# Two experts' rows kept on chip and added by TensorE; the other rows read back while the last expert runs

## Chip, core and metric

One NeuronCore of a Trainium2 chip runs the whole kernel in one launch. The metric is the device time of that launch in microseconds (us), the median of several runs. One further execution was taken with the hardware profiler; its rows are read here. TensorE is called PE, VectorE DVE, ScalarE ACT, GpSimd POOL and SyncE SP.

## What is computed

A two-layer encoder on 512 tokens of width 1024, all float32. Each layer mixes tokens (three kinds of attention and a convolution, one input and one output projection) and then runs a mixture of experts:

```python
for l in range(2):
    ...                                     # mixer: x = x + gt1 * mix
    h2 = rms_norm(x, g2) * (1 + sc2) + sh2
    # every token goes to 2 of 32 experts, with gates that sum to p_group
    y  = sum over its two experts e:  gate_e * ((silu(h2 @ Wg[e]) * (h2 @ Wu[e])) @ Wd[e])
    x  = x + gt2 * y
out = rms_norm(x, g_final)
```

Wg and Wu are 1024x512 and Wd is 512x1024, so one expert has three weights of 2 MB, and a layer reads 32 x 6 MB of them. That is most of the bytes that the kernel moves.

## The kernel before

**Tokens.** The tokens lie in four tiles of 128 (`TT` = 4) in `x`. After routing, each expert has a list of up to 128 (token, choice) slots. Experts with at most 64 tokens run at half width (`by_width`). Tokens that don't fit are handled by `on_overflow` branches, which aren't taken with these inputs.

**One expert.** POOL gathers its tokens from DRAM (`gather`), PE transposes them (`turn_tokens`), multiplies by gate and up weights (`gate_up`), DVE multiplies the two (`expert_hidden`), PE transposes that (`turn_hidden`) and multiplies by the down weight (`down`), DVE scales the two halves out of PSUM into `yexp[j]` (`expert_rows`), and POOL scatters these rows to `yexp_d` in DRAM (`scatter`). There are two buffers `yexp[j]`, for even and odd experts. PE's order at the end of a layer is `gate_up(30)`, `turn_tokens(31)`, `turn_hidden(30)`, `gate_up(31)`, `down(30)`, `turn_hidden(31)`, `down(31)`. Experts are counted from 0, so 30 and 31 are the last two.

**Weights.** SP issues all weight loads in one fixed order, in halves of 1 MB, into ten places: six slots of `ring`, and `home`, `hT`, `work` and some pieces (`PIECES`: parts of `arena`, `masks` and `gate`). A load is issued when PE has used what was in the place. The last six units of a layer are gate 30, up 30, gate 31, up 31, down 30, down 31. Behind them SP issues the first two loads of the next layer's input projection (line 818), and then `load_rows`.

**Combine.** When all scatters of the layer have landed, ACT and SP read the rows back as eight tiles of 512 KB: for each tile t of tokens the rows of the token's first expert (`yrow[t][0]`, "lower", into `work`) and of its second (`yrow[t][1]`, "upper", into `arena`). DVE adds them, gate times row, with one `scalar_tensor_tensor` of 128x1024 each (lines 2093 and 2096), and signals `x_done` per tile. ACT then squares the tile, DVE normalises it. After layer 0 the tiles are transposed and the next layer's first projection begins (line 1058). After layer 1 they are stored as the output. While it waits after layer 0, PE runs 16 products that nobody reads (`idle_products(16, 7)`, line 1114).

**Routing.** DVE's `route` makes the slot lists in small linked steps. Its second signal `slots_ready` lets PE compute the lists of the overflow blocks (`more_lists`), which stand in PE's queue ahead of `turn_tokens(0)` of the first expert; SP's load into `work` waits for the same signal.

## Time and profile before

| | us |
|---|---|
| median of 3 runs | 1784.95 |
| lowest, highest | 1782.51, 1791.69 |
| the profiled execution, its own time | 1786.48 |
| its span in the trace | 1784.6 |
| PE busy | 1584.0 (89%) |
| DVE busy | 715.8 (40%) |
| ACT busy | 435.2 (24%) |
| POOL busy | 160.1 (9%) |

The span starts at 0 and all positions below are us from it. The experts of layer 0 run from about 404 to 886 and those of layer 1 from about 1274 to 1758. Busy PE is a modelled figure; what matters in the rows is when an instruction starts, and what the engine waited for.

### The profile page before, as it was taken

The page shows a single profiled execution, that of the slowest core. Times are in us where ns is not written, and L with a number is a line of the kernel's source. Part 1 is how long each engine was busy: PE and PEld are TensorE (multiplying, and loading weights), DVE is VectorE, ACT ScalarE, POOL GpSimd, SP SyncE. Part 2 cuts the span into 40 slices and gives each one's busy share as a digit, 9 for nine tenths or more (in the row PEclk, how much of TensorE's full clock was granted, in tenths as well). Part 3 has the DMA queues.
Part 4 walks back from the last instruction along what each step waited for, and adds up shares of the span by engine and source line. Part 5 has one row for each costly group of instructions (what it writes and reads, how often), then busy time and mean ns, then how long its engine had stood idle before and what let it go on. Part 6 is the DMA issues. An engine that isn't in the chain of part 4 may idle for free.

```text
span 1784.6 us, 22330 instructions
## 1 busy us (share of the span) xinstructions
PE 1584.0 (89%) x7460; PEld 765.9 (43%) x7460; DVE 715.8 (40%) x1461; ACT 435.2 (24%) x995; POOL 160.1 (9%) x184
## 2 busy tenths in 40 slices
PE   5999999998998998878889999999899989887783
PEld 2455655463333343333345555455433333333331
DVE  1577476662222212212257855743422222212224
ACT  2111467112121111111121016741111112111111
POOL 0000000111111011111000000001110111111010
PEclk9999999989999999999999999999999999999997
DMA  9625633479999999999972355213899999999995
GB/s 361 237 71 189 212 116 106 152 311 360 405 398 403 407 405 399 411 409 415 371 273 95 135 195 210 69 48 122 321 400 404 402 412 401 408 413 403 396 409 191
DMA packets 124293, 528.44 MB, mean 296 GB/s; under 512 B 17184, under 2 KB 23328, under 8 KB 77568
## 3 DMA queue, kind: packets, MB, share of 16 engines
q1 hardware_dynamic: 106704, 491.46, 70.3%
q0 software_dynamic: 12480, 24.51, 4.3%
q10 hardware_dynamic: 4976, 10.55, 1.7%
q8 instruction: 100, 1.64, 0.4%
q14 instruction: 33, 0.27, 0.0%
HBM read 520.96 MB, written 23.86 MB: 305 GB/s over the span
## 4 chain that ended last, share of the span: by engine, by line
PE 68%; DMA 14%; ACT 5%; DVE 5%; SPq 4%; issue 4%; ACTq 0%; DVEq 0%; POOLq 0%
PE ps L1424 28%; PE ps L1058 18%; DMA ring<-in_w_exp_up 10%; PE ps L1271 6%; PE ps L1422 4%; PE ps L1213 2%; ACT arena L1701 2%; PE ps L1227 2%; SPq L873 2%; SPq L863 2%; PE ps L1253 2%; ACT arena L1715 1%; DMA ring<-in_w_in 1%; PE ps L1084 1%; PE ps L1397 1%
## 5 line engine op out<-in xcount | busy, mean ns | idle before, releaser
L1424 PE MATMUL ps<-ring,arena 128*64 128x512 f32 x1728 | 490.6, 609 | 53.5 <-ACT arena L1715 29.9
L1424 PEld LDWEIGHTS ps<-ring,arena 128*64 128x64 f32 x1728 | 157.9, 140 | 282.4 <-issue 266.5
L1058 PE MATMUL ps<-ring,hT 128*128 128x512 f32 (+1 forms) x768 | 254.3, 486 | 1.4 <-DVE z L1868 0.9
L746 DVE TENSOR_TENSOR arena<-ps,arena 64x512 f32<-64x512 f32 (+1 forms) x64 | 44.3, 693 | 459.4 <-ACT arena L1709 380.9
L1709 ACT ACTIVATE arena<-ps 128x512 f32<-128x512 f32 x64 | 38.2, 597 | 756.3 <-PE ps L1424 705.5
L1058 PEld LDWEIGHTS ps<-ring,hT 128*128 128x128 f32 x768 | 144.0, 190 | 100.9 <-issue 90.7
L754 DVE TENSOR_TENSOR arena<-ps,gate 64x512 f32<-64x512 f32 (+1 forms) x64 | 43.7, 683 | 280.2 <-PE ps L1424 260.2
L1023 POOL DMA_INDIRECT yexp_d<-arena,masks x64 | 59.7, 932 | 836.2 <-DVE arena L756 774.0
L1424 PE MATMUL ps<-home,arena 128*64 128x512 f32 x304 | 115.6, 601 | 11.2 <-ACT arena L1715 5.1
L1424 PE MATMUL ps<-hT,arena 128*64 128x512 f32 x272 | 104.6, 602 | 9.7 <-DMA work<-in_w_exp_up 4.9
L1424 PE MATMUL ps<-work,arena 128*64 128x512 f32 x288 | 106.7, 595 | 7.1 <-ACT arena L1715 5.1
L1271 PE MATMUL ps<-ring,hT 128*128 128x512 f32 x256 | 112.5, 595 | 0.0
L1701 ACT ACTIVATE arena<-ps,modc 128x128 f32<-128x128 f32 x256 | 96.5, 457 | 36.9 <-PE ps L1397 33.0
L1424 PE MATMUL ps<-arena 128*64 128x512 f32 x216 | 84.8, 596 | 10.0 <-ACT arena L1715 5.3
L1857 DVE SCALAR_TENSOR_TENSOR work<-z,small,work 128x512 f32<-128x512 f32 x120 | 90.0, 751 | 3.9
L735 DVE TENSOR_SCALAR arena<-ps,modc 128x128 f32<-128x128 f32 x256 | 87.5, 404 | 7.4 <-PE ps L1397 5.0
L1397 PEld LDWEIGHTS ps<-cst,arena 128*128 128x128 f32 x512 | 62.3, 194 | 49.3 <-issue 49.3
L1455 PE MATMUL ps<-cst,arena 128*128 128x128 f32 x256 | 48.2, 311 | 30.5 <-DVE arena L746 19.4
L1397 PE MATMUL ps<-cst,arena 128*128 128x128 f32 x512 | 73.7, 287 | 0.0
L1213 PE MATMUL ps<-arena 64*128 64x512 f32 (+1 forms) x256 | 72.6, 647 | 0.6 <-ACT arena L1607 0.6
L1271 PEld LDWEIGHTS ps<-ring,hT 128*128 128x128 f32 x256 | 47.9, 190 | 57.1 <-issue 57.1
L1013 POOL DMA_INDIRECT arena<-xn_d,masks x64 | 62.3, 974 | 37.6 <-issue 18.4
(233 smaller groups left out, 1735.7 us busy)
## 6 DMA issues: line engine op xcount, KB each, us to landing
ring<-in_w_exp_up SPq DMA_DIRECT2D x80, 1024.0 KB, 23.7
ring<-in_w_exp_down SPq DMA_DIRECT2D x78, 1024.0 KB, 24.4
ring<-in_w_exp_gate SPq DMA_DIRECT2D x74, 1024.0 KB, 24.2
ring<-in_w_ada SPq DMA_DIRECT2D x24, 2048.0 KB, 10.4
ring<-in_w_in SPq DMA_DIRECT2D x8, 2048.0 KB, 21.5
home<-in_w_exp_gate SPq DMA_DIRECT2D x14, 1024.0 KB, 27.3
home<-in_w_exp_up SPq DMA_DIRECT2D x12, 1024.0 KB, 28.4
hT<-in_w_exp_down SPq DMA_DIRECT2D x12, 1024.0 KB, 24.1
```

The source lines that it names most:

```text
L735: last = dve.tensor_scalar(xgT[:, k, :], ps[:, 4, P * q:P * q + P], modc[:, 3, k:k + 1], modc[:, 2, k:k + 1], ALU.mult, ALU.add)
L1013: pool.indirect_dma_start(xg[e % 2][0:w, :], None, xn2_d[l], bass.IndirectOffsetOnAxis(ap=gidx[0:w, e:e + 1], axis=0), bounds_check=last_t ...
L1023: pool.indirect_dma_start(yexp_d[l], bass.IndirectOffsetOnAxis(ap=lst[0:w, e:e + 1], axis=0), yexp[e % 2][0:w, :], None, bounds_check=last ...
L1058: last = pe.matmul(out, lhs(k), rhs(k), start=(k == 0), stop=(k == n - 1))
L1213: fills(pe.matmul(bank(key), qkT[g][p0:p0 + n, hp, P * t:P * t + P], qkT[g][p0:p0 + n, 2 + hp, :], start=True, stop=True, tile_position=(p ...
L1271: last = pe.matmul(bank(key), yT[:, k, P * t:P * t + P], slot(unit)[:, k, :], start=(k == K_OUT[0]), stop=(k == K_OUT[-1]))
L1397: last = pe.transpose(bank_e(b).rearrange("p (a s) -> p a s", a=4)[:, q, :], xg[j][:, k:D:KD], ident)
L1422: last = [pe.matmul(outs[c], lhs(k), rhs(c, k), start=(k == 0), stop=(k == n - 1)) for c in range(2)]
L1424: last = [pe.matmul(outs[c][HALF * c:HALF * c + HALF, :], lhs(k)[:, 0:HALF], rhs(c, k), start=(k == 0), stop=(k == n - 1), tile_position=( ...
L1455: last = pe.transpose(ps[:, 2, P * c:P * c + P], hid[:, c:DE:KE], ident)
L1701: last = act.activation(xgT[:, q, :], ps[:, 3, P * q:P * q + P], ACT.Identity, scale=modc[:, 3, q:q + 1], bias=modc[:, 2, q:q + 1])
L1857: ins = dve.scalar_tensor_tensor(conv[f], z[:, f, k:k + S], w, conv[f], ALU.mult, ALU.add)
```

## The change

It keeps the rows of experts 30 and 31 in the two buffers `yexp[0]` and `yexp[1]`, and does not scatter them.

- A matrix `select` (in `z`) is made near the start of a layer's experts. It holds, for each of the two experts, in row = slot and column = token, the gate of that slot. After `down(31)` PE multiplies its transpose with the rows: 16 matmuls of 128x128 by 128x512 into four banks, two for each of eight (tile, half) pairs. DVE adds each result to `x` with a `tensor_tensor` of 128x512.
- The 30 other experts' rows are read back by SP, which waits for their scatters and for the last uses of `work` and `home`, behind the last weight loads and ahead of the next layer's first loads. `upper` now lies in `home`. DVE adds them in `add_rows(t)`: tiles 0 and 1 ahead of `expert_hidden(31)`, tile 2 between `expert_rows(30)` and `expert_rows(31)`, tile 3 after it.
- Rows that are no longer written would be undefined, so `yexp_d` is filled with finite numbers first: two copies of `x`'s 2 MB from DRAM to DRAM, issued by SP behind the output projection's loads. POOL waits for them ahead of its first scatter.
- `route` computes gates that are zero for experts 30 and 31, and the select matrix's inputs; `slots_ready` is signalled after these steps instead of after `slot_of_rank`.
- PE's idle products between the layers go from 16 to 4.

```diff
+        upper = home[:, :, :].rearrange("p k n -> p (k n)").rearrange("p (t d) -> p t d", t=TT)
+        yrow = [(lower[t], upper[:, t, :]) for t in range(TT)]
+        select = z[:, :, HALO:HALO + S]
...
@@ route
-            slot_of_rank().then_inc(slots_ready, 1)
+            link(slot_of_rank())
 
             dve.wait_ge(rexp_ready, 2 * (l + 1))
             link(dve.tensor_reduce(rt[:, pgrp:pgrp + TT], r3(diff), AX_X, ALU.add))
...
                 link(dve.tensor_tensor(gates[:, i, :], parts[2 * i], parts[2 * i + 1], ALU.add))
+            ends, kept2 = slot_val[:, :, NE - 2:NE], rt[:, 36:36 + 2 * TT]
+            flat_gates = gates[:, :, :].rearrange("p k t -> p (k t)")
+            first_block = view(z, 356, [[W, P], [NBLK, 2 * TT]])
+            link(dve.tensor_tensor(kept2, flat_gates, first_block, ALU.mult))
+            link(dve.tensor_tensor(over_gates[:, :], flat_gates, kept2, ALU.subtract))
+            dve.tensor_tensor(ends, hot.rearrange("p k t e -> p (k t) e")[:, :, NE - 2:NE],
+                              view(z, 236, [[W, P], [1, 2 * TT], [0, 2]]), ALU.mult).then_inc(slots_ready, 1)
+            link(dve.tensor_scalar(flat_gates, rt[:, e01:e01 + 2 * TT], NE - 2.5, None, ALU.is_lt))
+            link(dve.tensor_tensor(flat_gates, flat_gates, kept2, ALU.mult))
...
+                link(dve.tensor_copy(last_gate[:, :], bank((l, "more_lists"))[:, NE - 2:NE]))
                 link(slot_lists((l, "more_lists"), NE, P))
                 dve.sem_inc(more_ready, 1)
+                for t in range(TT):
+                    last = dve.tensor_scalar(last_token[:, :, t], gidx[:, NE - 2:NE], -P * t, None, ALU.add)
+                link(last)
...
@@ experts_dve
+            def last_selects():
+                for i in range(2):
+                    for t in range(TT):
+                        ins = dve.tensor_scalar(select[:, i, P * t:P * t + P], C["iota"], last_token[:, i, t:t + 1],
+                                                last_gate[:, i:i + 1], ALU.is_equal, ALU.mult)
+                ins.then_inc(select_ready, 1)
+            def add_rows(t):
+                dve.wait_ge(lower_in[t], 16 * (l + 1))
+                link(dve.scalar_tensor_tensor(x[:, t, :], yrow[t][0], gates[:, 0, t:t + 1], x[:, t, :], ALU.mult, ALU.add))
+                dve.wait_ge(yrow_in[t], 16 * (l + 1))
+                link(dve.scalar_tensor_tensor(x[:, t, :], yrow[t][1], gates[:, 1, t:t + 1], x[:, t, :], ALU.mult, ALU.add))
...
             expert_tokens(1, 1)
+            last_selects()
             expert_rows(0, 0, 0)
...
+            for t in range(2):
+                add_rows(t)
             expert_hidden(NE - 1, HE - 1, 1)
             expert_rows(NE - 2, HE - 1, 0)
+            add_rows(2)
             expert_rows(NE - 1, HE - 1, 1)
+            add_rows(3)
+            dve.sem_inc(rows_added, 1)
...
@@ SP
-                    if l and n == 2:
-                        load_rows(l - 1)
-                        sp.wait_ge(yrow_in[TT - 2], 16 * l)
-                        sp.wait_ge(yrow_in[TT - 1], 16 * l)
...
+                for k in range(2):
+                    sp.dma_start(yexp_d[l].rearrange("(k s) d -> k s d", k=2)[k], a["x"].rearrange("b s d -> (b s) d")).then_inc(fill_out, 16)
                 for m, u in ADA_NEXT[l]:
                     load_ada(m, u)
...
                 for m in (0, 1, 3, 4, 2, 5):
                     expert_unit(NE // TURN, m)
 
+                for j in range(2):
+                    sp.wait_ge(yrow_out[j], 16 * (HE - 1) * (l + 1))
+                await_expert_used(l, *last_expert(l, WORK))
+                await_expert_used(l, *last_expert(l, HOME))
+                for t in range(TT):
+                    load_rows(l, 0, t, lower_in[t])
+                    load_rows(l, 1, t, yrow_in[t])
...
@@ POOL
-                for e in range(NE):
-                    if e + 2 < NE:
-                        gather(e + 2)
+                pool.wait_ge(fill_out, 32 * (l + 1))
+                for e in range(NE - 2):
+                    gather(e + 2)
                     scatter(e)
...
@@ PE
-                    idle_products(16, 7)
+                    idle_products(4, 3)
...
+                pe.wait_ge(select_ready, l + 1)
+                pe.wait_ge(drained[5], expert_bank(l, 5) + NE)
+                pe.wait_ge(drained[6], expert_bank(l, 6) + NE)
+                for t in range(TT):
+                    for h in range(2):
+                        key = (l, "last_rows", t, h)
+                        await_free(pe, key)
+                        for i in range(2):
+                            last = pe.matmul(bank(key), select[:, i, P * t:P * t + P], yexp[i][:, 512 * h:512 * h + 512],
+                                             start=(i == 0), stop=(i == 1))
+                        fills(last, key)
...
@@ ACT, combine
-                for t in range(TT):
-                    act.dma_start(yrow[t][0], yv[t, 0]).then_inc(lower_in[t], 16)
-                act.wait_ge(yrow_out[1], 16 * HE * (l + 1))
-                for t in range(1, TT, 2):
-                    act.dma_start(yrow[t][1], yv[t, 1]).then_inc(yrow_in[t], 16)
...
@@ DVE, after the experts
                 for t in range(TT):
-                    dve.wait_ge(lower_in[t], 16 * (l + 1))
-                    link(dve.scalar_tensor_tensor(x[:, t, :], yrow[t][0], gates[:, 0, t:t + 1], x[:, t, :], ALU.mult, ALU.add))
-                for t in range(TT):
-                    dve.wait_ge(yrow_in[t], 16 * (l + 1))
-                    dve.scalar_tensor_tensor(x[:, t, :], yrow[t][1], gates[:, 1, t:t + 1], x[:, t, :], ALU.mult, ALU.add)\
-                        .then_inc(x_done, 1)
+                    for h in range(2):
+                        key, xh = (l, "last_rows", t, h), x[:, t, 512 * h:512 * h + 512]
+                        await_filled(dve, key)
+                        link(dve.tensor_tensor(xh, bank(key), xh, ALU.add))
+                        dve.sem_inc(drained[bank_of[key][0]], 1)
+                    dve.sem_inc(x_done, 1)
```

## Rows read from the trace of the kernel before

**Rows 1.** Page, 40 slices of the span: DMA busy tenths and GB/s.
```profile
DMA  9625633479999999999972355213899999999995
GB/s 361 237 71 189 212 116 106 152 311 360 405 398 403 407 405 399 411 409 415 371 273 95 135 195 210 69 48 122 321 400 404 402 412 401 408 413 403 396 409 191
```

**Rows 2.** Chain that ended last, layer 0's end: start us, us, what.
```profile
846.38 21.75 DMA ring<-in_w_exp_up
...
880.98 6.57 DMA yexp_d<-arena,masks
...
888.90 10.43 DMA work<-yexp_d
...
900.74 1.30 DVE x L2096
```

**Rows 3.** The same chain, end of layer 1.
```profile
1758.52 6.55 DMA yexp_d<-arena,masks
...
1765.16 4.78 DMA arena<-yexp_d
```

**Rows 4.** Timeline, layer 0's end: start us, us, engine, line, what [idle before].
```profile
876.04 0.69 DVE L746 TENSOR_TENSOR arena<-ps,arena 64x512 f32<-64x512 f32 x1 [8.04 <-PE ps L1424]
...
878.72 0.75 PE L1455 MATMUL ps<-cst,arena 128*128 128x128 f32 x4
...
885.10 0.69 DVE L756 TENSOR_TENSOR arena<-ps,gate 64x512 f32<-64x512 f32 x1
...
895.62 2.60 DVE L2093 SCALAR_TENSOR_TENSOR x<-work,gates,x 128x1024 f32<-128x1024 f32 x2 [0.69 <-DMA work<-yexp_d]
...
908.72 3.67 PE L1058 MATMUL ps<-ring,hT 128*128 128x512 f32 x8
```

**Rows 5.** Timeline, end of layer 1.
```profile
1750.97 0.75 PE L1455 MATMUL ps<-cst,arena 128*128 128x128 f32 x4
...
1757.07 0.69 DVE L756 TENSOR_TENSOR arena<-ps,gate 64x512 f32<-64x512 f32 x1
...
1771.35 1.06 ACT L1522 ACTIVATE arena<-x 128x1024 f32<-128x1024 f32 x1 [16.68 <-DVE x L2096]
...
1781.06 0.48 DVE L1775 SCALAR_TENSOR_TENSOR x<-x,rstd,rT 128x256 f32<-128x256 f32 x1
```

**Rows 6.** Timeline, issues by SP and POOL near both ends.
```profile
861.07 16.29 SPq L818 DMA_DIRECT2D ring<-in_w_in  x2
...
1730.17 2.14 SPq L863 DMA_DIRECT2D gate<-in_w_exp_down  x1
...
1731.89 0.93 POOL L1023 DMA_INDIRECT yexp_d<-arena,masks  x1 [15.93 <-DVE arena L756]
```

**Rows 7.** DMA view of these three issues alone: KB each, us to landing.
```profile
ring<-in_w_in SPq DMA_DIRECT2D x1, 2048.0 KB, 24.7
...
gate<-in_w_exp_down SPq DMA_DIRECT2D x1, 512.0 KB, 22.6
yexp_d<-arena,masks POOLq DMA_INDIRECT x1, 7.9
```

**Rows 8.** One line's view, L2071: ns least, median, most.
```profile
L2071 DVE TENSOR_TENSOR work<-ps,gate x16: 680/692/693, 338.9 to 1245.6; 128x512 f32<-128x512 f32 x16
```

**Rows 9.** Timeline, start of layer 1's experts.
```profile
1267.01 1.22 DVE L651 TENSOR_TENSOR arena<-cst,z 128x1024 f32<-128x1024 f32 x1
...
1269.61 2.32 PE L1058 MATMUL ps<-arena 128*128 128x96 f32 x16
...
1269.84 0.36 DVE L714 TENSOR_TENSOR gates<-z 128x4 f32<-128x4 f32 x2
```

**Rows 10.** Timeline of PE after a stall and without one, layer 1.
```profile
1714.04 1.02 PE L1424 MATMUL ps<-ring,arena 128*64 128x512 f32 x1 [2.59 <-DMA hT<-in_w_exp_up]
...
1725.92 3.65 PE L1424 MATMUL ps<-work,arena 128*64 128x512 f32 x16 [0.84 <-ACT arena L1715]
```

**Rows 11.** Windows: us, busy us (instructions) of each engine, PEclk, DMA share, GB/s.
```profile
1714.00:1717.00 3.00, 2.96 (x8) 0.94 (x10) 0.00 (x0) 0.00 (x0) 1.65 (x2) 0.53 1.02 423
```

More of the change, by code:

```diff
@@ L291, in plan_banks @@
             used[b] += NE
+        for t in range(TT):
+            for h in range(2):
+                take((l, "last_rows", t, h), (0, 1, 2, 7)[2 * (t % 2) + h])
     return at
@@ L347, in program @@
             + [probsT[:, :, :, :].rearrange("p a t q -> p (a t q)"), tmp[:, :, :].rearrange("p a s -> p (a s)")]
-        yrow = [(lower[t], xs[:, t, :]) for t in range(TT)]
+        upper = home[:, :, :].rearrange("p k n -> p (k n)").rearrange("p (t d) -> p t d", t=TT)
+        yrow = [(lower[t], upper[:, t, :]) for t in range(TT)]
+        select = z[:, :, HALO:HALO + S]
+        last_gate = sb("last_gate", [P, 2])
+        over_gates = sb("over_gates", [P, 2 * TT])
+        last_token = sb("last_token", [P, 2, TT])
         rT = sb("rT", [P, 2, P])
@@ L458, in program @@
         yrow_out = [sem(f"yrow_out{j}") for j in range(2)]
+        fill_out, select_ready = sem("rows_filled"), sem("select_ready")
+        over_rows = [sem(f"over_rows_in{l}") for l in range(DEPTH)]
+        over_added = [sem(f"over_rows_added{l}") for l in range(DEPTH)]
+        rows_added = sem("rows_added")
         lower_in = [sem(f"lower_rows_in{t}") for t in range(TT)]
@@ L790, in experts_dve @@
                     dve.wait_ge(over_pe[l], 4 * n + 4)
-                    dve.tensor_tensor(yexp[0], ps[:, 5:7, :].rearrange("p b n -> p (b n)"), gate[:, 1, :], ALU.mult).then_inc(over_dve[l], 1)
+                    dve.tensor_tensor(over_y, ps[:, 5:7, :].rearrange("p b n -> p (b n)"), gate[:, 1, :], ALU.mult).then_inc(over_dve[l], 1)
+                dve.wait_ge(over_rows[l], 16 * 2 * TT)
+                for k in range(2):
+                    for t in range(TT):
+                        dve.scalar_tensor_tensor(x[:, t, :], yrow[t][k], over_gates[:, TT * k + t:TT * k + t + 1], x[:, t, :],
+                                                 ALU.mult, ALU.add).then_inc(over_added[l], 1)
+                    dve.wait_ge(over_added[l], TT * (k + 1))
         block = ctx.enter_context(nc.Block())
@@ L829, in _, with load_rows @@
                     sp.dma_start(x[:, :, :], a["x"].rearrange("b (t p) d -> p (b t) d", p=P)).then_inc(x_in, 16)
-            def load_rows(l):
-                with on_overflow(sp, l):
-                    sp.wait_ge(over_out[l], 16 * NE * (NBLK - 1))
-                for j in range(2):
-                    sp.wait_ge(yrow_out[j], 16 * HE * (l + 1))
-                yv = yexp_d[l].rearrange("(k t p) d -> t k p d", k=2, p=P)
-                for t in range(0, TT, 2):
-                    sp.dma_start(yrow[t][1], yv[t, 1]).then_inc(yrow_in[t], 16)
+            def load_rows(l, k, t, landed):
+                sp.dma_start(yrow[t][k], yexp_d[l].rearrange("(k t p) d -> t k p d", k=2, p=P)[t, k]).then_inc(landed, 16)
             for l in range(DEPTH):
@@ L855, in _ @@
                     load(unit, slot(unit), a["w_out"][l].rearrange("(k p) n -> p k n", p=P)[:, :, 512 * n:512 * n + 512])
+                for k in range(2):
+                    sp.dma_start(yexp_d[l].rearrange("(k s) d -> k s d", k=2)[k], a["x"].rearrange("b s d -> (b s) d")).then_inc(fill_out, 16)
                 for m, u in ADA_NEXT[l]:
@@ L877, in await_first_free @@
                     if b == HOME and l:
+                        sp.wait_ge(x_done, TT * l)
                         await_expert_used(l - 1, *last_expert(l - 1, b))
@@ L927, in _ @@
                     expert_unit(NE // TURN, m)
+                for j in range(2):
+                    sp.wait_ge(yrow_out[j], 16 * (HE - 1) * (l + 1))
+                await_expert_used(l, *last_expert(l, WORK))
+                await_expert_used(l, *last_expert(l, HOME))
+                for t in range(TT):
+                    load_rows(l, 0, t, lower_in[t])
+                    load_rows(l, 1, t, yrow_in[t])
                 with on_overflow(sp, l):
@@ L937, in _ @@
                     sp.wait_ge(over_pe[l], 4 * NE * (NBLK - 1))
-            load_rows(DEPTH - 1)
+                    sp.wait_ge(over_out[l], 16 * NE * (NBLK - 1))
+                    sp.wait_ge(rows_added, l + 1)
+                    for k in range(2):
+                        for t in range(TT):
+                            load_rows(l, k, t, over_rows[l])
             for t in range(TT):
@@ L1508, in _ @@
                         last.then_inc(over_pe[l], 1)
+                pe.wait_ge(select_ready, l + 1)
+                pe.wait_ge(drained[5], expert_bank(l, 5) + NE)
+                pe.wait_ge(drained[6], expert_bank(l, 6) + NE)
+                for t in range(TT):
+                    for h in range(2):
[5 more added lines that the diff above has]
+                        fills(last, key)
         @block.scalar
@@ L1746, in _ @@
                         act.activation(hidT.rearrange("p c s -> p (c s)"), ps[:, 2, :], ACT.Copy).then_inc(over_act[l], 1)
-                with on_overflow(act, l):
-                    act.wait_ge(over_out[l], 16 * NE * (NBLK - 1))
                 combine(l)
```

18 lines of the change are left out of this document (9 added, 9 removed).

## The prediction

> **What bounds the kernel now.** I read the page's slices first. In the slices in which the experts run, DMA is at 9 tenths and moves 398 to 418 GB/s [rows 1]: a layer reads 201 MB of weights, and that stream sets the pace. Over the mixer it falls to 48 to 212 GB/s. Next the chain. It reaches layer 0's last experts through a weight load of 21.75 us [rows 2], most of which is waiting in the queue. Behind the last expert it goes through a scatter (6.57 us), the read-back (10.43 us) and DVE's adds [rows 2]. Layer 1 ends in the same way, with 6.55 and 4.78 us [rows 3]. These two serial stretches are what the change attacks. From the timeline I take four instants. DVE's last `expert_rows` half ends at 885.10 + 0.69 = 885.8 in layer 0 [rows 4] and at 1757.8 in layer 1 [rows 5]. The first finished tile (`x_done`) is there at 900.74 + 1.30 = 902.0 [rows 2], and in layer 1 when ACT starts on it, 1771.3 [rows 5]. So a layer spends 16.2 and 13.5 us from its last row to its first finished tile.
>
> **Part 1, the tail that goes.** After the change these 16.2 and 13.5 us hold what DVE has in its queue behind `expert_rows(31)`: `add_rows(3)`, two adds of 1.3 us (the linked pair took 2.60 [rows 4]), the overflow branch, which I estimate at 0.3, and two PSUM adds of 128x512. The nearest operation of that shape, also out of PSUM, took 0.69 [rows 8]; with its link 0.73. Together 2.6 + 0.3 + 1.46 = 4.4 us. PE's first four of 16 row matmuls take 1.8 us (16 in 3.65 is 0.23 for half-width ones that run two at a time, so 0.43 to 0.46 each [rows 10]) and hide behind `add_rows(3)`; the other 12 run while DVE goes through its tiles. Savings if nothing else moves: 16.2 - 4.4 = 11.8 in layer 0, 13.5 - 4.4 = 9.1 in layer 1.
>
> **Part 2, the following tiles.** Before, a tile cost DVE one add of 1.3 us after the first; now it costs two of 0.73. Before layer 1's projection three tiles must be done, after layer 1 all four, so +0.5 and +0.8 with the waits for links. The span from the first tile to DVE's last instruction (1771.3 to 1781.5 [rows 5]), and the stores behind it, are otherwise the same. In layer 0, PE's projection starts at 908.7 [rows 4], 6.7 behind `x_done`; ACT's and DVE's normalising sets that, so that fewer idle products gain nothing there.
>
> **Part 3, where the rows come from.** This is where I differ from the change's idea. `add_rows(0)` and `add_rows(1)` stand ahead of `expert_hidden(31)` on DVE, and PE cannot pass `turn_hidden(31)` without that. In the queue of DVE behind the wait are `expert_hidden(31)` and `expert_rows(30)`; PE waits for the one and, for free banks, for the other. So the question is when 2 MB (tiles 0 and 1, both choices) have landed. SP issues them behind the last weights. In the kernel before, the next thing behind the last weights is the first load of line 818, also 2 MB. It was issued at 861.07 and landed 24.7 us later, at 885.8 [rows 6, 7]: at full rate 2.1 MB take 5.1 us, so nearly 20 of the 24.7 were spent behind the weights ahead of it. The rows take its place, so tile 1's second half lands at 885.8, however early SP issues it. Its scatters are no obstacle: the last one needed left at 1731.9 in layer 1 and took 7.9 us, so 1739.8 [rows 6, 7], with the weights still in flight. In layer 1 the last weight piece was issued at 1730.17 and landed after 22.6 us, at 1752.8 [rows 6, 7]; 2.1 MB more at 410 GB/s [rows 1] is 5.1 us, so 1757.9.
>
> From there: last add 1.3, `expert_hidden(31)` 0.69 [rows 4], links and signal 0.15. PE's `turn_hidden(31)` starts at 888.0 instead of 878.7 [rows 4] and at 1760.0 instead of 1751.0 [rows 5]: **+9.3 and +9.0 us** of PE standing still. What follows it (`turn_hidden`, ACT's copy, `down(31)`, `expert_rows(31)`) moves with it. Tiles 2 and 3 land 5 us later still, which is before their adds. After a wait of only 2.59 us PE came back at half clock: granted 0.53 in 1714 to 1717, that is 1.2 instead of 2.4 GHz, and 8 matmuls in these 3 us, where 16 take 3.65 at full clock [rows 10, 11]. A stall of 9 us will do that, and `down(31)` has 16 such matmuls: between 0 and 1.8 us, I take **+1.5** per layer.
>
> The Trainium skill's page "DMA: Bandwidth & Descriptors", in its rules for kernel authors, advises to issue a DMA early, compute, and wait for it late, since then the fixed cost overlaps; the same page fits 2.0 us plus bytes at 436 GB/s to a transfer (an estimate for 2.1 MB from it: 6.8 us). By that the rows, issued well ahead of `expert_hidden(31)`, would be there in time. The line 818 load of the same size contradicts it with 24.7 us, because the queue ahead was full. That page's case is the first rival below, with its time from rows.
>
> **Part 4, the start of the experts.** `slots_ready` used to fire at 1267.01 + 1.22 = 1268.2. PE was then still in idle products and began `more_lists` at 1269.61 [rows 9]. Now it fires after all of the gate steps (the last at 1269.84 + 0.36 = 1270.2 [rows 9]), a link more (0.1), and three new steps of about 0.2, so at 1270.9. PE waits 1.3 us more, `turn_tokens(0)` and the first expert start that much later, the first weight place is freed that much later, and since DMA is at its limit from then on, the end of the layer moves too. Layer 0 has the same steps: **+1.3 twice**. Bounds: 0 if slack at the start takes it up, 2 if the clock comes back later too. The other new DVE steps (copy, offsets, eight `select` pieces of 128x128) I estimate at 3 us: a piece is an eighth of the 1.22 us operation [rows 9], 0.15, plus 0.1 for each instruction. They lie where DVE waits for PE in the first expert; DVE is busy 40% of the span. Free; without that cover they would cost their 3 us per layer.
>
> **Part 5, the fill.** 4 MB more through DMA per layer. It is issued behind the output projection's weights, where the slices show 106 to 116 GB/s in layer 0 and 48 to 135 in layer 1 [rows 1], long ahead of POOL's first scatter. If it came in the saturated stretch, it would cost 4.2 MB at 410 GB/s, 10 us a layer. I take 0. The two loads of line 818 now follow 4 MB of rows, 10 us later at about 896 and 901, still ahead of PE's projection.
>
> **The sum.** Layer 0: +9.3 + 1.5 - 11.8 + 0.5 = -0.5. Layer 1: +9.0 + 1.5 - 9.1 + 0.8 = +2.2. Start of experts: +2.6. Total +4.3. The profiled execution took 1786.48 and would take 1790.8; it stands 1.5 above the median, so from 1784.95 I get **1789.3 us**. A change under 0.5% (8.9 us) can hardly be told from none.
>
> **The rivals.**
> - *The rows are there in time* (the idea of the change, and the page's). Then +9.3, +9.0 and twice 1.5 vanish: 4.3 - 21.3 = -17.0, 1768 us. It needs the rows to pass the weights that were issued ahead of them, or the queue to be emptier. For it: the early scatters, and DMA that is only partly used in the last slices. Against it: 24.7 us [rows 7]. A partial version (lateness halved) would give about 1778. Chance of either 0.15.
> - *The rows land still later*, and it is slower. Place: the wait in `add_rows(1)`. Before, read-backs of 4 MB alone took 10.43 us on the chain [rows 2], near full rate, but behind weights on the engine that is furthest behind. Each us that the 2 MB come later costs two (both layers). From 2.3 us later per layer on it is slower by more than 0.5%; at 4 us later 1797. Chance 0.2.
> - *The gain goes unseen because the start of the experts eats it*: the 1.3 us there could be up to 2 per layer, +1.4 in all, 1791. It only shifts within the likeliest case.
> - The likeliest, stall about as long as the tail that goes: 0.65, own range 1783 to 1796.
>
> **Range and chances.** 1778 to 1798, which leaves out most of the first rival and the far end of the second. Faster by over 0.5%: 0.14. Within: 0.66. Slower: 0.20.
>
> **What would show it.** In the changed kernel: SP's row loads issued before 870 and landing only near 886; DVE idle ahead of the adds of tile 1; a wait of 8 to 10 us ahead of `turn_hidden(31)` put down to DVE, in both layers; PE's granted clock at 0.5 in the last `down`; 4 to 5 us from the last `expert_rows` half to the first finished tile; `more_lists` 1.3 us later behind DVE. The prediction is wrong if `turn_hidden(31)` starts without that wait, or if the fill runs into the weights.

## The result, and the profile after

The changed kernel is slower by 1.3%. Its median is 1810.08 us (4 runs), beside 1787.48 us for the kernel before (4 runs); the ratio is 1.013, with a 95% interval of 1.0104 to 1.0155. (One of the four took 3309.85 us, far outside of everything else, and is left out of the ratio.) The prediction was 1789.3 us with a range of 1778 to 1798 and 0.66 on no change: it missed by 21 us and the range does not hold the time. (Its base of 1784.95 was the median of three runs of the kernel before; a fourth, of 1790.01, moved that median up by 2.5 us.)

The page of the changed kernel: span, DMA busy tenths, GB/s.

```profile
span 1807.7 us, 22478 instructions
...
DMA  9625643389999999999952358213799999999993
GB/s 360 230 70 199 243 161 115 145 324 363 405 386 403 416 404 398 413 407 414 382 181 94 129 197 300 68 48 144 293 395 404 402 411 406 405 413 395 407 406 135
```

The experts' slices are as before [rows 1]: DMA at 9 tenths and about 405 GB/s. The span is 23.1 us longer. So the stream of weights still sets the pace inside a layer, and nearly all of the time was lost at its ends. The timeline of the changed kernel at layer 0's end (start, us, engine, line, what, idle before it and who ended that):

```profile
869.14 0.33 SPq L888 DMA_DIRECT2D work<-yexp_d  x1
...
885.80 1.28 DVE L799 SCALAR_TENSOR_TENSOR x<-work,gates,x 128x1024 f32<-128x1024 f32 x1 [14.00 <-DMA work<-yexp_d]
...
891.56 0.69 DVE L775 TENSOR_TENSOR arena<-ps,arena 64x512 f32<-64x512 f32 x1 [0.51 <-DVE x L801]
...
892.31 1.13 PE L1516 MATMUL ps<-cst,arena 128*128 128x128 f32 x4 [9.73 <-DVE arena L775]
...
894.20 6.37 PE L1485 MATMUL ps<-ring,arena 128*64 128x512 f32 x16 [0.76 <-ACT arena L1780]
...
901.32 0.69 DVE L785 TENSOR_TENSOR arena<-ps,gate 64x512 f32<-64x512 f32 x1
...
902.27 13.97 PE L1579 MATMUL ps<-arena,z 128*128 128x512 f32 x32 [1.69 <-DVE arena L785]
...
905.55 1.53 DVE L2158 TENSOR_TENSOR x<-ps,x 128x512 f32<-128x512 f32 x2 [1.02 <-issue]
...
916.07 3.60 PE L1175 MATMUL ps<-cst 128*128 128x512 f32 x8
...
919.51 1.95 PE L1134 MATMUL ps<-cst,arena 128*128 128x128 f32 x16
...
922.38 4.10 PE L1119 MATMUL ps<-ring,hT 128*128 128x512 f32 x9 [0.93 <-DVE hT L1850]
```

Read it from the top. SP issues the first rows at 869.14. DVE stands 14.00 us for them, makes the four adds of tiles 0 and 1, and only then the hidden multiply (L775). PE waits 9.73 us for that (L1516) and then runs the last `down` in 6.37 us instead of 3.65. Then comes the row that the prediction had wrong: **the 16 row products take 13.97 us** (L1579). The row counts x32 for these 16 `matmul` calls: the profile has two instructions for each float32 `matmul`, which I call passes from here on, and one for each `transpose` (x4 for the four of `turn_hidden`). Behind them stand the idle products (L1175), the transposes (L1134) and the next layer's projection (L1119), with no wait between the first three and 0.93 us ahead of the projection. PE's queue, not DVE, now sets when layer 1 begins. The same places in layer 1 (1791.56 is when ACT takes the first finished tile):

```profile
1776.94 1.13 PE L1516 MATMUL ps<-cst,arena 128*128 128x128 f32 x4 [8.38 <-DVE arena L775]
...
1785.63 0.69 DVE L785 TENSOR_TENSOR arena<-ps,gate 64x512 f32<-64x512 f32 x1
...
1786.58 13.97 PE L1579 MATMUL ps<-arena,z 128*128 128x512 f32 x32 [1.70 <-DVE arena L785]
...
1791.56 1.06 ACT L1595 ACTIVATE arena<-x 128x1024 f32<-128x1024 f32 x1 [11.21 <-DVEq L2160]
```

The chain that ended last, both layers (start, us, what): where the chain of before went through scatter, read-back and adds [rows 2, 3], it now goes through the wait for rows and through the products.

```profile
869.14 16.64 DMA work<-yexp_d
...
902.27 13.97 PE ps L1579 x32
...
1755.27 15.15 DMA work<-yexp_d
...
1786.58 13.99 PE ps L1579 x32
```

And the start of layer 1's experts (DVE, then PE), to be held against [rows 9]:

```profile
1284.30 0.17 DVE L734 TENSOR_TENSOR arena<-work,z 128x16 f32<-128x16 f32 x1
...
1284.53 2.94 PE L1119 MATMUL ps<-arena 128*128 128x98 f32 x16 [2.10 <-DVE arena L734]
```

PE has run out of idle products and waits 2.10 us for the step that now carries `slots_ready`; its list products (16 passes) then take 2.94 us instead of 2.32.

From these instants the 23.1 us can be cut into pieces. Each is the difference of a stretch between the same two instructions, after minus before:

| stretch | layer 0 | layer 1 | sum | predicted |
|---|---|---|---|---|
| up to the first `gate_up` of the experts | +2.4 | +2.6 | +5.0 | +2.6 |
| first `gate_up` to `turn_tokens(31)` | +1.4 | +1.5 | +2.9 | 0 |
| `turn_tokens(31)` to `turn_hidden(31)`: the stall | +9.8 | +8.2 | +18.0 | +18.3 |
| `turn_hidden(31)` to the last row half | +2.6 | +2.6 | +5.2 | +3.0 |
| last row half to the next projection, or to the end | -2.6 | -5.5 | -8.1 | -19.6 |
| all | +13.7 | +9.4 | +23.1 | +4.3 |

The last line is rounded: the pieces of layer 0 add to +13.6. The stall is as predicted. The largest error, 11.5 of 18.8 us, is in the tail, which gives back 8.1 us and not 19.6.

The table is of one execution. The same cuts through a0_after, the same kernel again, give +7.2 for the starts, +19.0 for the second and third lines together (here +20.9), +3.9 for the fourth and -8.2 for the tails, +22.0 in all. So the tails repeat to 0.1 us, and the small lines differ by up to 2 us from one execution to the next.

### The profile page after: what moved, and what is told of

The parts are those of the page before. It is cut to its first block, busy times and chain, and to the rows that moved or that the text cites. A ratio compares the mean times of both kernels' runs of the same rounds, so it can differ in the third digit from the quotient of the medians.

```text
span 1807.7 us, 22478 instructions
## 1 busy us (share of the span) xinstructions
PE 1607.5 (89%) x7500; PEld 774.7 (43%) x7500; DVE 733.8 (41%) x1513; ACT 435.5 (24%) x995; POOL 157.4 (9%) x180
## 2 busy tenths in 40 slices
DMA packets 124165, 536.57 MB, mean 297 GB/s; under 512 B 16989, under 2 KB 23133, under 8 KB 77312
## 4 chain that ended last, share of the span: by engine, by line
PE 61%; DMA 16%; SPq 9%; DVE 5%; issue 4%; ACT 4%; ACTq 0%; DVEq 0%
PE ps L1485 22%; PE ps L1119 18%; DMA ring<-in_w_exp_up 8%; SPq L921 7%; PE ps L1332 6%; DMA arena<-in_w_exp_up 3%; PE ps L1274 2%; PE ps L1483 2%; PE ps L1288 2%; DMA work<-yexp_d 2%; PE ps L1314 2%; PE ps L1579 2%; DMA work<-in_w_exp_up 1%; DMA ring<-in_w_in 1%; ACT arena L1766 1%
## 5 line engine op out<-in xcount | busy, mean ns | idle before, releaser
L1485 PE MATMUL ps<-ring,arena 128*64 128x512 f32 x1728 | 497.6, 617 | 55.8 <-ACT arena L1780 31.3
L1119 PE MATMUL ps<-ring,hT 128*128 128x512 f32 (+1 forms) x768 | 254.3, 486 | 4.1 <-DMA ring<-in_w_in 2.3
L775 DVE TENSOR_TENSOR arena<-ps,arena 64x512 f32<-64x512 f32 (+1 forms) x64 | 44.3, 693 | 436.1 <-ACT arena L1774 378.8
L1119 PEld LDWEIGHTS ps<-ring,hT 128*128 128x128 f32 x768 | 144.0, 190 | 103.4 <-issue 91.3
L1485 PE MATMUL ps<-arena 128*64 128x512 f32 x216 | 89.0, 626 | 9.9 <-ACT arena L1780 6.5
L1516 PE MATMUL ps<-cst,arena 128*128 128x128 f32 x256 | 48.8, 315 | 48.6 <-DVE arena L775 37.0
```

Source lines behind the costliest of these rows:

```text
L1119: last = pe.matmul(out, lhs(k), rhs(k), start=(k == 0), stop=(k == n - 1))
L1485: last = [pe.matmul(outs[c][HALF * c:HALF * c + HALF, :], lhs(k)[:, 0:HALF], rhs(c, k), start=(k == 0), stop=(k == n - 1), tile_position=( ...
L1516: last = pe.transpose(ps[:, 2, P * c:P * c + P], hid[:, c:DE:KE], ident)
```

## The experiments

Three theories stood against each other. **Theory A** is the ledger above: DVE's wait for rows ahead of the hidden multiply costs some 18 us, with a slower last `down` behind it; 14 us of products on PE eat most of the saved tail; the later signal costs most of the rest. **Rival B**: the added DMA traffic (the pages count 536.57 MB instead of 528.44; the fill adds 8.4, and two experts' scatters are gone) slows the stream of weights, and the ends only show it. **Rival C**: the rows are late because SP's queue serves them last, and another queue would have them in time. The changed kernel itself was run again beside the first four.

**a0_after: the changed kernel.** 

> The changed kernel once more, on the chip of the runs beside it, as their base: about 1808 to 1812 us, 22 to 25 above the kernel before. Theory: four places make that, as read from its trace against that of before: the DVE wait for rows ahead of the last experts' hidden product (9.8 and 8.2 us), the half clock behind it (2.6 twice), the 16 row products, which are 14.0 us on PE, with 3.4 us of idle products behind them (8.6 in layer 0, 3.0 in layer 1), and the later signal for the overflow lists (1.5 to 2.5 per layer); the shorter tail gives back 11.1 and 8.5.

Measured: 1809.58 us, ratio 1.0129 (1.011 to 1.0148), span 1806.6. The products take 13.97 us again, from 901.53, and the next projection starts at 921.48. It is the base for the experiments below.

**e1_no_idle: no idle products between the layers.** The changed kernel without one line:

```diff
-                    idle_products(4, 3)
```

> The changed kernel without the 4 idle products between the layers. Theory (PE is the bound behind the last expert, since 16 row products take 14.0 us and the idle ones stand in its queue): first projection of layer 1 starts 3.4 us earlier, kernel 3.4 us faster. Rival (DVE and ACT set the pace, as my prediction had it): no change, 0 to 0.5 us.

Measured: 1805.75 us, ratio 1.0105 (1.0084 to 1.0127), so 3.8 us less than a0_after in the medians, though the two intervals overlap; the rows carry the reading. Its timeline of PE at layer 0's end:

```profile
901.21 13.97 PE L1578 MATMUL ps<-arena,z 128*128 128x512 f32 x32 [1.69 <-DVE arena L785]
...
917.74 4.53 PE L1119 MATMUL ps<-ring,hT 128*128 128x512 f32 x10 [0.76 <-DVE hT L1849]
```

From the first product to the projection it is 16.5 us, where a0_after has 19.95. Taking 3.4 us of work that nobody reads out of PE's queue brings the projection 3.4 us forward: PE is what this stretch waits for. The prediction had said that fewer idle products gain nothing there.

**e2_hidden_first: DVE makes the hidden values before it waits for any row.**

```diff
-            for t in range(2):
-                add_rows(t)
             expert_hidden(NE - 1, HE - 1, 1)
             expert_rows(NE - 2, HE - 1, 0)
-            add_rows(2)
+            add_rows(0)
             expert_rows(NE - 1, HE - 1, 1)
-            add_rows(3)
+            for t in range(1, TT):
+                add_rows(t)
```

> The changed kernel with DVE's order changed at the end of a layer: expert_hidden(31), expert_rows(30), add_rows(0), expert_rows(31), add_rows(1 to 3). Theory (the wait for the rows ahead of expert_hidden(31) is what holds PE): the 9.7 and 8.4 us of idle PE ahead of turn_hidden(31) vanish in both layers, the clock stays full in the last down, and down(31) ends some 12 and 11 us earlier. The adds of tiles 1 to 3 then lie behind the last expert, 8 us, beside 14 us of row products, so that 3 to 6 us per layer come back: 10 to 18 us faster than the changed kernel. Rival (PE would have waited anyway, for the last down weights or a free bank): under 4 us.

Measured: 1793.44 us, ratio 1.0042 (1.0028 to 1.0057), 16.1 us less than a0_after. PE and DVE at layer 0's end, from its timeline:

```profile
882.36 0.74 PE L1515 MATMUL ps<-cst,arena 128*128 128x128 f32 x4
884.23 3.65 PE L1484 MATMUL ps<-ring,arena 128*64 128x512 f32 x16 [1.12 <-DVE arena L785]
...
890.18 8.80 PE L1578 MATMUL ps<-arena,z 128*128 128x512 f32 x16 [2.29 <-DVE arena L785]
899.55 7.13 PE L1578 MATMUL ps<-arena,z 128*128 128x512 f32 x16 [0.57 <-DVEq L2158]
...
912.67 2.81 PE L1118 MATMUL ps<-ring,hT 128*128 128x512 f32 x6 [0.77 <-DVE hT L1849]
```

```profile
885.60 1.28 DVE L799 SCALAR_TENSOR_TENSOR x<-work,gates,x 128x1024 f32<-128x1024 f32 x1 [1.76 <-DMA work<-yexp_d]
```

The stall is gone: `turn_hidden(31)` starts at 882.36 with no wait, and with it the slow `down` (3.65 us again). The rows come when they came before, at 885.6. They were not the trouble; what stood behind them in DVE's queue was. The gain is 16.1 and not the 23.2 of stall and slow `down`, because six adds of 1.28 us now stand between the last row half and the first add from PSUM, and in their turn hold PE: its second 16 passes wait for DVE to free banks (0.57, DVEq L2158).

**e3_half_products: expert 31's products only.** This kernel leaves out the rows of expert 30, which are neither scattered nor added.

```diff
-                        for i in range(2):
-                            last = pe.matmul(bank(key), select[:, i, P * t:P * t + P], yexp[i][:, 512 * h:512 * h + 512],
-                                             start=(i == 0), stop=(i == 1))
+                        last = pe.matmul(bank(key), select[:, 1, P * t:P * t + P], yexp[1][:, 512 * h:512 * h + 512],
+                                         start=True, stop=True)
```

> The changed kernel with only the second of the two row products of each tile half (expert 30's rows are left out of the result): 8 products instead of 16, 7.0 us of PE instead of 14.0. Theory (PE's products pace the tail): first projection of layer 1 starts 6 to 7 us earlier and layer 1 ends 2 to 4 us earlier, together 8 to 11 us. Rival (DVE's adds and norms pace it): under 2 us.

Measured: 1801.37 us, ratio 1.0089 (1.0071 to 1.0107), 8.2 us less than a0_after. PE, layer 0's end:

```profile
902.34 3.67 PE L1578 MATMUL ps<-arena,z 128*128 128x512 f32 x8 [1.69 <-DVE arena L785]
906.43 3.76 PE L1578 MATMUL ps<-arena,z 128*128 128x512 f32 x8 [0.41 <-DVEq L2158]
...
916.18 4.10 PE L1119 MATMUL ps<-ring,hT 128*128 128x512 f32 x9 [0.76 <-DVE hT L1849]
```

13.8 us from the first product to the projection, 6.1 less than a0_after's 19.95, for 7 us of products less. Eight products are 16 passes here. Against the kernel before, layer 0's tail gives back 8.8 us (a0_after 2.7) and layer 1's 7.1 (5.5). With e1 this shows that the products' length on PE is what the tail of layer 0 costs.

**e4_warm_stall: ten idle products ahead of `turn_hidden(31)`,** so that PE is not still while it waits.

```diff
+                idle_products(10, 7)
```

> The changed kernel with 10 idle products (8.7 us at full clock) in PE's queue between down(30) and turn_hidden(31), where PE stands still for 9.7 and 8.4 us. Theory (the standing still drops PE's clock, and the last down then takes 6.4 instead of 3.7 us): granted clock stays at full, down(31) takes about 3.7 us, and each layer is 2 to 2.6 us shorter, 4 to 5 us together; in layer 1 the products can outlast the stall by 0.3 us. Rival (the last down is slow for another cause, such as its weights): no gain, or up to 1 us slower.

Measured: 1805.31 us, ratio 1.0102 (1.0077 to 1.0126). That is 4.3 us less than a0_after, but it ran on another chip and the intervals overlap, so the time tells little; the rows tell more. PE's timeline, and windows of layer 0's end (us, then busy us and instructions of PE, PE's loads, DVE, ACT and POOL, granted clock, DMA share, GB/s):

```profile
884.71 8.85 PE L1175 MATMUL ps<-cst 128*128 128x512 f32 x20
894.46 0.75 PE L1516 MATMUL ps<-cst,arena 128*128 128x128 f32 x4 [0.90 <-DVE arena L775]
896.09 5.35 PE L1485 MATMUL ps<-ring,arena 128*64 128x512 f32 x16 [0.89 <-DVE arena L785]
```

```profile
894.00:896.00 2.00, 0.75 (x4) 0.56 (x4) 1.94 (x4) 0.60 (x1) 0.00 (x0) 1.00 0.95 364
896.00:898.00 2.00, 1.91 (x6) 0.83 (x8) 1.97 (x2) 1.49 (x2) 0.00 (x0) 0.57 1.04 392
```

A surprise. The transposes now run at full clock (0.75 us, not 1.13), but the `down` behind them still takes 5.35 us: after two pauses of 0.9 us the granted clock falls to 0.57 in 896 to 898, the lower of the two levels (1.2 of 2.4 GHz) for most of that stretch. From `turn_hidden(31)` to the last row half it is 8.4 us in both layers. The changed kernel has 9.7 and 9.4, a0_after 8.8 and 8.9, the kernel before 7.1 and 6.8. Four other runs that keep the stall and have no such products (e1, e3, e5, e10) take 8.3 to 9.6. So beside the 0.4 us of the transposes no gain from the warm products is shown. That PE was still during the wait is not the whole cause of the slow `down`; what else lowers the clock there these runs don't tell.

**e5_act_queue: ACT issues the row loads,** behind its copy of expert 30's turned hidden values; SP goes on with the next layer's loads.

```diff
-                for t in range(TT):
-                    load_rows(l, 0, t, lower_in[t])
-                    load_rows(l, 1, t, yrow_in[t])
...
+                for t in range(TT):
+                    act.dma_start(yrow[t][0], yv[t, 0]).then_inc(lower_in[t], 16)
+                    act.dma_start(yrow[t][1], yv[t, 1]).then_inc(yrow_in[t], 16)
```

> The changed kernel with the eight row loads issued by ACT on its own DMA queue, behind ACT's copy for expert 30, instead of by SP behind the last weights. Theory (the rows land late because they stand behind queued weights on SP's rings): from issue to landing 8 to 13 us instead of 16.6 to 19.8, tile 1 is there some 5 us earlier, the stall ahead of turn_hidden(31) shrinks from 9.7 to 3 to 6 us, unless the last down weights are now delayed past it; 4 to 12 us faster in all. Rival (the rows are slow by themselves, by their 4 KB pieces or by DRAM): landing again after 17 us or more, no gain.

Measured: 1805.66 us, ratio 1.0114 (1.0089 to 1.0138): 3.9 us less than a0_after, on another chip and with intervals that overlap. The first and the last of DVE's four adds of tiles 0 and 1, and the DMA view of 870 to 880 (queue, packets, MB, share of 16 engines):

```profile
878.83 1.28 DVE L799 SCALAR_TENSOR_TENSOR x<-work,gates,x 128x1024 f32<-128x1024 f32 x1 [7.38 <-DMA work<-yexp_d]
...
889.39 1.28 DVE L801 SCALAR_TENSOR_TENSOR x<-home,gates,x 128x1024 f32<-128x1024 f32 x1 [1.86 <-DMA home<-yexp_d]
```

```profile
q1 hardware_dynamic: 598, 3.06, 74.7%
q10 hardware_dynamic: 274, 1.03, 25.9%
```

The first rows do come sooner (adds from 878.83 instead of 885.80), but the fourth add starts at 889.39, as late as in the changed kernel (889.77), and `turn_hidden(31)` at 891.92. PE's wait ahead of it is 8.68 us in layer 0 and 6.71 in layer 1, where the changed kernel has 9.73 and 8.38; 3 to 6 were expected. ACT's queue (q10) gets a quarter of the bytes of these 10 us and, from the same view of 878 to 880, about half (0.41 of 0.82 MB) once it runs. Rival C falls: another queue does not have the rows there in time. In 870 to 880 the engines are full, and the second queue takes its bytes out of the same 410 GB/s. The section "Issuing engines are not separate DMA queues" in the Trainium skill's page "DMA: Bandwidth & Descriptors" says that DMAs issued from the scalar, sync or gpsimd engine run on the same 16 DMA engines and interleave; the trace agrees, with 3.06 and 1.03 MB in 10 us.

**e10_act_queue_alone: as e5, with SP's next-layer loads held until the rows have landed.** It asks whether those loads, which e5 issues from 864.65 on, were what the rows shared with.

```diff
+                for t in range(TT):
+                    sp.wait_ge(yrow_in[t], 16 * (l + 1))
```

> The changed kernel with the row loads on ACT's queue, and SP's loads for the next layer held back until all rows have landed. With the loads not held back, tile 1 landed only at 889.4 in layer 0 (889.8 in the changed kernel), though its issue to first landing was 7.8 us. If the next layer's loads took the bandwidth, tile 1 now lands 3 to 6 us earlier and the kernel is 3 to 8 us faster than with them. If the last weights took it, nothing changes but for what the held loads cost (0 to 3 us slower).

Measured: 1806.88 us, ratio 1.0115 (1.0097 to 1.0134). DVE's fourth add, and the DMA views of 880 to 882 and of 888 to 890:

```profile
887.96 1.28 DVE L801 SCALAR_TENSOR_TENSOR x<-home,gates,x 128x1024 f32<-128x1024 f32 x1 [1.81 <-DMA home<-yexp_d]
```

```profile
q10 hardware_dynamic: 145, 0.51, 63.7%
q1 hardware_dynamic: 41, 0.31, 37.4%
...
q10 hardware_dynamic: 117, 0.41, 50.7%
```

That is 1.4 us earlier than in e5, and no faster in all. So most of the rows' time was not due to the next layer's loads. The last experts' own weights, which SP's queue (q1) still moved beside them, are not the whole of it either: by 888 to 890 SP's queue moves nothing, and ACT's moves 0.41 MB in 2 us, less than its 0.51 MB beside the weights, with the DMA engines half busy (50.7%). In the kernel before, the same queue moved 0.70 MB in 2 us (890 to 892). What holds the rows to this pace in e10 the runs don't tell, so that e5's rival, rows that are slow by themselves, is not excluded.

**e6_before_late_slots: the kernel before, with `slots_ready` signalled after the gate steps** and three more small ones of the same kind (their values aren't used).

```diff
-            slot_of_rank().then_inc(slots_ready, 1)
+            link(slot_of_rank())
...
+            for _ in range(2):
+                link(dve.tensor_tensor(kept2, flat_gates, view(z, 356, [[W, P], [NBLK, 2 * TT]]), ALU.mult))
+            dve.tensor_tensor(kept2, flat_gates, view(z, 356, [[W, P], [NBLK, 2 * TT]]), ALU.mult).then_inc(slots_ready, 1)
```

> The kernel before with one part of the change alone: the second slots_ready comes after the gate steps and three small further ones, as in the changed kernel. Theory: PE waits 1.2 to 2.1 us ahead of the overflow lists, the experts start that much later, and the end moves by as much: 2.5 to 4 us slower. Rival (the weight stream, not PE, sets the pace from the start and takes it up): 0 to 1 us.

Measured (11 runs): 1793.21 us, ratio 1.0038 (1.0026 to 1.005), so +6.7 us, where 2.5 to 4 were expected, for a signal that comes 2.7 us later in each layer. Layer 0's first `gate_up` comes 1.2 us later. That of layer 1 comes 3.8 later, of which 0.9 stood already at the layer's first projection. PE, start of layer 1's experts:

```profile
1265.79 2.82 PE L1119 MATMUL ps<-cst 128*128 128x512 f32 x6
1272.40 2.62 PE L1063 MATMUL ps<-arena 128*128 128x96 f32 x16 [3.79 <-DVE z L719]
```

The six passes end at 1268.6, PE stands 3.79 us, and in 1274 to 1276 the granted clock is 0.50. In the kernel before, the idle products reached past the signal [rows 9]; past their end, a later signal costs the wait and the clock. The two starts are 1.2 and 2.9, together 4.1 of the 5.5 us by which this trace's span is longer. The rest arose elsewhere: the stretches from the first `gate_up` to `turn_hidden(31)` are 0.9 and 1.8 longer, the tails 1.2 shorter. e7 below has 1.5 and 1.5 in the same stretches at an unchanged time, so that I don't put these to the signal.

**e7_before_fill: the kernel before, with the two fill copies and POOL's wait.**

```diff
+                for k in range(2):
+                    sp.dma_start(yexp_d[l].rearrange("(k s) d -> k s d", k=2)[k], a["x"].rearrange("b s d -> (b s) d")).then_inc(fill_out, 16)
...
+                pool.wait_ge(fill_out, 32 * (l + 1))
```

> The kernel before with one part of the change alone: the two copies of 2 MB per layer into the rows' DRAM buffer, with POOL's wait for them. Theory (they run while DMA is little used): within 1 us of the kernel before. Rival (they delay loads of the mixer or of the first weights): 2 to 6 us slower, which would be the part of the loss that my list leaves open (1.4 and 1.5 us of drift within the experts, 0.9 in the first mixer).

Measured (12 runs): 1785.17 us, ratio 0.9992 (0.998 to 1.0003). 4 MB a layer from DRAM to DRAM cost nothing where they are put. That takes the fill out of rival B. For the rest of B the table leaves at most its second line, 2.9 us. And that line is not shown to be the change's: from the first `gate_up` to `turn_hidden(31)` this trace too is 1.5 and 1.5 us longer than that of the kernel before, while e2, e8 and e9, which have the fill and the row products, are at +0.3 to -0.7 there.

**e8_fixes: what the runs point to.** The order of e2, no idle products between the layers, and five instead of three idle products ahead of the slot lists.

```diff
-                    idle_products(4, 3)
...
-                idle_products(3, 1)
+                idle_products(5, 1)
```

> The changed kernel with DVE's new order (as in the run that put expert_hidden(31) first), without the 4 idle products between the layers, and with 5 instead of 3 idle products ahead of the overflow lists, so that PE doesn't stand still there. From the runs so far: the changed kernel at 1809.6, less 16.1 for the order, 3.8 for the idle products, and 1 to 4 if PE's clock then stays full at the start of the experts: 1786 to 1789, about the kernel before. Rival (the two savings overlap, since both end in the same products): 1790 to 1793.

Measured (12 runs): 1787.95 us, ratio 1.0009 (0.9999 to 1.0019): the time of the kernel before. PE, layer 0's end:

```profile
891.16 8.80 PE L1577 MATMUL ps<-arena,z 128*128 128x512 f32 x16 [3.89 <-DVE arena L785]
900.52 7.13 PE L1577 MATMUL ps<-arena,z 128*128 128x512 f32 x16 [0.56 <-DVEq L2157]
```

Its stretches, as in the table above: the starts cost 3.2 and 1.5 us; from there to the last row half it is 1.9 in layer 0, where DVE's wait for tile 0 holds `expert_rows(31)`, and 0.2 in layer 1; the tails give back 3.6 (19.3 us from the last row half, at 890.90, to the projection, at 910.21, instead of 22.9) and 1.7. In all +1.4 by its span of 1786.0. A tail of scatter, read-back and adds was exchanged for one of six adds and two blocks of products that is 2 to 4 us shorter. The starts take most of that back, though not all by the later signal: of layer 0's 3.2 us, 1.6 stood already when the idle products ahead of the lists began (396.57 instead of 394.93).

**e9_fixes_early: e8's order, and `slots_ready` as early as in the kernel before,** with three idle products ahead of the lists and none between the layers. It leaves out the routing step for experts 30 and 31's gates, so that their rows are added with wrong factors.

```diff
-            link(slot_of_rank())
+            slot_of_rank().then_inc(slots_ready, 1)
...
-            dve.tensor_tensor(ends, hot.rearrange("p k t e -> p (k t) e")[:, :, NE - 2:NE],
-                              view(z, 236, [[W, P], [1, 2 * TT], [0, 2]]), ALU.mult).then_inc(slots_ready, 1)
```

> New order and no idle products between the layers, and the second slots_ready signalled behind slot_of_rank as in the kernel before; the step that puts the gates of experts 30 and 31 into the lists' input is left out, so that their rows are added with wrong factors. Theory (the later signal costs what it cost in the kernel before, 6.7 us): 1781 to 1785, some 2 to 5 us faster than the kernel before. Rival (the signal's cost was mostly chance in the weight stream): 1788 to 1791.

Measured (11 runs): 1785.41 us, ratio 0.999 (0.998 to 1.0001), 2.5 us less than e8 and not to be told from the kernel before. The lists start at 402.25 and 1269.27, the latter as before at 1269.61; the former is 2.1 later than before, and its idle products began 2.1 later too. So if the gate step could be had without delay, these repairs would still reach no gain that can be told from none.

## Why the prediction was wrong

**Right: the stall (part 3).** Rows behind a full queue: the first was issued at 869.14 and landed at 885.8, the fourth, issued at 870.47, at 889.5. From the DMA view of the changed kernel, these two issues (KB, us to landing):

```profile
work<-yexp_d SPq DMA_DIRECT2D x1, 512.0 KB, 16.6
...
home<-yexp_d SPq DMA_DIRECT2D x1, 512.0 KB, 19.0
```

I had tile 1 at 885.8 in a stream that now runs 3.8 us later, which is 889.6. +9.8 and +8.2 us of stall against +9.3 and +9.0, and e2 shows that they were the wait's. That the weights ahead of the rows alone made the wait is not shown (e10). The rows were issued 16.7 us ahead of the first add, and DVE still stood idle for 14.00 of these. The advice in the Trainium skill's page "DMA: Bandwidth & Descriptors" (rules for kernel authors), to issue early, compute and wait late, which the prediction weighed, was not enough here, as these rows show.

**Wrong: the size of the products (part 1), and with it who sets the tail (part 2).** This is the step that failed: "PE's first four of 16 row matmuls take 1.8 us (16 in 3.65 is 0.23 for half-width ones that run two at a time, so 0.43 to 0.46 each [rows 10])", and "the other 12 run while DVE goes through its tiles". I doubled 0.23 for the two half-width ones side by side and stopped there; each float32 product is two passes of 0.44, so 16 take 13.97 us and not 7. The number stood in the trace of before, in the idle products of the same shape (timeline of the kernel before, PE), 16 calls:

```profile
884.29 14.00 PE L1114 MATMUL ps<-cst 128*128 128x512 f32 x32
```

The row of `down` that I went by has the same two: its x16 are the passes of 8 calls, not 16 calls [rows 10]. With 14.0 us for the products the sum for layer 0's tail would have been: products to 13.8 us after they start, idle products 3.4, transposes and copy 2.9, and 0.3 before, 20.4 us against 22.9, so -2.6 and not -11.3. Layer 1's first tile came nearly as I had it (-8.4 against -9.1), and then the tiles followed at PE's pace, 3.4 us each: +2.9 where I had +0.8. Together 11.5 of the 18.8 us. e1 (-3.8 for 4 idle products) and e3 (-8.2 for half of the products) show it. e3 is also the test of my own price: with 7 us of products the tails gave back 8.8 and 7.1, not 11.3 and 8.3. So the price is most of the error, and the rest is part 2's, which had DVE and ACT and not PE's queue set layer 0's tail.

**First finished tile (part 1).** 5.1 and 5.2 us after the last row half, 4.4 forecast. DVE stood 1.02 us ahead of the adds from PSUM, where the overflow branch is; I had estimated 0.3.

**Start of the experts (part 4).** Right in kind, +5.0 instead of +2.6. In layer 1 the lists do begin 1.3 us later, counted from the layer's first projection, as forecast. The other 1.3 is the clock, to which I gave no price beyond a bound: PE waits 2.10 us and then runs at granted 0.50 in 1286 to 1288, so that the lists take 2.94 us instead of 2.32 and the transposes behind them 1.81 instead of 1.06. In layer 0 the lists begin 2.3 later, but 0.85 of that stood already when the idle products ahead of them began (395.78 instead of 394.93), and ACT's instructions are 0.8 late from 147.73 on (146.98 before), far ahead of `route`. In e6 the late signal alone costs 4.1 us at the two starts of its trace.

**The last `down` (part 3).** +2.6 twice (2.0 on average in a0_after) where I had taken 1.5 of a range to 1.8. I had priced `down` by a short stall [rows 10, 11], behind which the granted clock was back at 1.00 in 1718 to 1720. Here the transposes ran slowly too (1.13 for 0.75), and `down` took 6.37 us for 3.65, nearly all of it at the lower level. Windows of the changed kernel, columns as above:

```profile
896.00:898.00 2.00, 2.00 (x8) 0.67 (x6) 0.20 (x1) 0.00 (x0) 0.00 (x0) 0.50 1.06 384
898.00:900.00 2.00, 2.00 (x8) 0.47 (x4) 0.00 (x0) 0.00 (x0) 0.00 (x0) 0.57 1.07 369
```

**The fill (part 5).** 0 forecast, 0 measured (e7).

**The rivals.** "The rows are there in time" did not happen. Nor did "still later": the slower outcome came by a mechanism that I had not priced, PE as the bound of the tail. I had reasoned that PE idles there and so has room; the stretch was idle in the kernel before because PE had nothing to do, and 14 us of work do not fit into a wait that the change itself shortens to 5. One reading was off without weight: the slices of the experts in [rows 1] are 396 to 415 GB/s, not 398 to 418.

**Open.** The 1.4 and 1.5 us between each layer's first `gate_up` and `turn_tokens(31)`, for which neither a wait nor a transfer showed up, and which e7 has at an unchanged time. The lag of layer 0 ahead of the lists: it is 0.9 to 4.4 us in the traces of all kernels with the fill and -0.3 in e6, which has none, while e7's time says that the fill costs nothing. The pace of ACT's queue in e10. And why the clock fell in e4.

## What to carry to other kernels

Read the price of a new operation from the row of the same shape and type, and look at its count: a row that says x32 for 16 calls gives the price of a call. When a change turns a wait into work for an idle engine, lay that engine's whole queue end to end up to the next thing that others wait for, since the removed wait was also its cover. And place a wait for a transfer behind, not ahead of, whatever in the same queue feeds the engine that sets the pace: putting the hidden multiply and the rows of expert 30 ahead of the four adds was worth 16 us here, more than any other single edit.

## What the hardware showed that I had not expected

- A second DMA queue did not hurry its transfers past a full first one: in 10 us it moved 1.03 of 4.1 MB, and the first 512 KB landed after 7.8 us, but the eighth only after 23.1 us (e5). With the first queue empty it was no faster: 0.41 MB in 2 us, with the DMA engines half busy (e10).
- Keeping PE busy during a wait did not keep its clock: after 8.85 us of products at granted 1.00 and two pauses of 0.9 us, the next 2 us ran at 0.57 (e4). Without them, in the changed kernel, they ran at 0.50.
- A signal 2.7 us later in each layer cost 1.2 us at one start and 2.9 at the other. In the second PE ran at granted 0.50 behind the wait, and the transposes took 1.91 us instead of 1.06 (e6).
